# A wider spacing of threshold-search steps between the evictions of an in-projection

## Chip, core and metric

One NeuronCore of one Trainium2 chip runs the whole program. The metric is the device time of one execution in microseconds (us). Five engines matter. TensorE multiplies into PSUM. ScalarE and VectorE empty PSUM and do arithmetic, GpSimd does arithmetic on SBUF, and SyncE mostly issues transfers. Each engine executes its own instructions strictly in the order of its program, and semaphores are the only tie between engines: an instruction that waits holds up everything queued behind it on its engine.

## What is computed

One decoder layer on 1024 prompt tokens and 8 x 4 sample tokens. The part that the change touches is the in-projection `h @ w_in` and the choice of keys for sparse attention. The reference, cut:

```python
au, av, q, k, v, qi, ki, wi = jnp.split(h @ w_in, IN_SPLITS, axis=-1)
u = jax.nn.gelu(au); vg = layer_norm(jax.nn.gelu(av), a_ln_g, a_ln_b)
...
s = jax.nn.relu(jnp.einsum('bthd,bsd->bths', qi, ki_all))
score = jnp.einsum('bths,bth->bts', s, wi)
score = jnp.where(adm[None], score, -jnp.inf)
_, sel = lax.top_k(score, topk)          # topk = 256
```

The kernel doesn't sort. For each row of scores it looks for the threshold above which 256 keys lie, by 32 halvings, and turns the result into a mask.

## The kernel before

**Tiles and stages.** The prompt is cut into 8 tiles of 128 tokens (0 to 7), the 32 sample tokens are tile 8. The stage in question first makes the index projections and the scores of all tiles, and then projects tile after tile, in the order 8, 0, 1, ... 7 (`TURN`), by four groups of matmuls each: av (group 0), au (1), kv (2) and q (3). A group is 8 float32 products of 128x128 by 128x512 (16 rows of the profile), at L678, into one PSUM bank. Groups alternate between two banks, so group n+2 waits until ScalarE has evicted group n.

**Evictions, on ScalarE.** av goes to `vg` (L867), au to `u` (L873), kv to `k_nat` and `v_nat` (L878, L879), q to `mixT` (L884). ScalarE also evicts the spatial product `mix` of the tile before (`spat`, L904) and two transposes, `aT` and `kpost` (L785), and issues the loads of `ada_b` (L801) for a second product, `ada`, that runs in between (L708).

**GpSimd** normalises `vg` of each tile (the last line L565), multiplies `u` by `spat`, and rotates k and q. TensorE's `mix` of tile t (L691), one tile later, needs the normalised `vg` of t.

**The batched search.** The scores of tiles 2 to 7 are searched together. One step (`try`) needs both engines. VectorE counts the scores above the candidate `cand` for four tiles (L980), ScalarE does so for the other two with a Sign that accumulates (`near`, L896, two instructions, 128x768 and 128x1024). VectorE then waits for both counts, compares them with the bounds (L983), corrects (L984, L985) and writes the next candidate (L987), on which ScalarE's next Sign waits. So 32 steps are one serial chain. Behind it VectorE finishes the thresholds (`end`, L993 to L996) and turns the scores into masks (`pick`, 7 instructions for each of 6 tiles, L1004 to L1016). The attention stage's first VectorE instruction (L1097) stands behind all that.

**What sets the order.** A list `ORDER` is made once, and TensorE, ScalarE and VectorE each walk through it and emit their own part of every entry. For the stretch in question it is made from `LATE`, the groups and what belongs to them, by an account of time: `COST` adds 6.9 for a group, 2.0 for `mix`, 0.6 for `aT`, 0.4 for `kpost` and 1.0 for `ada`, and when the account holds enough for a step of the search, that step is put into the list there. These numbers only set the order; no engine waits for a time. TensorE has no part in `try`, `end` and `pick`.

Of the kernel before, what the change touches and what calls it, by code (L numbers as in the profile page):

```python
# [107 lines left out]
def step_kernel(nc, a, outs):  # L108
# [20 lines left out]
    with ExitStack() as keep, ExitStack() as tail:  # L129
# [117 lines left out]
        with ExitStack() as ctx:  # L247
# [85 lines left out]
            queue = [("try", 0, i) for i in range(SEARCH)] + [("end", 0, 0)]  # L333
            queue += [("pick", t, i) for t in range(2, TILES) for i in range(PICK)]
            began, time = False, 0.0
            for x in LATE:
                ORDER.append(x)
                began = began or x[0] == "ready"
                if began:
                    time += COST.get(x[0], 0.0)  # L340
                while queue and time >= (4.0 if queue[0][0] == "try" else 1.3):
                    time -= 4.0 if queue[0][0] == "try" else 1.3
                    ORDER.append(queue.pop(0))
            ORDER += queue + [("mix", TILES - 1, 0), ("kpost", TILES - 1, 0), ("aT", TILES - 2, 0)]
            NA = len(ORDER)
# [1894 lines left out]
```

How the kernel before makes its waits and increments, by code:

```python
                @block.sync  # L398
                def _(sp):
                    sp.dma_start(cnat[0:1, :], a["c_prompt"]).then_inc(s_c, 16)
                    sp.dma_start(cnat[1:1 + SEQS, :], a["c_sample"]).then_inc(s_c, 16)
                    sp.dma_start(const[:, :], a["table"]).then_inc(s_const, 16)
                    sp.wait_ge(s_z, 1)
                    for j in range(4):
                        sp.dma_start(modn[32 * j:32 * j + 1 + SEQS, 0, :],
                                     b_ada[j * 512:(j + 1) * 512].partition_broadcast(1 + SEQS)).then_inc(s_bada, 16)
# [9 lines left out]
                        sp.dma_start(bsp_s[s * DSEQ:(s + 1) * DSEQ, :],  # L416
                                     a["b_spatial"][0, :, 0:DSEQ].rearrange("h t -> t h"),
                                     allow_slow_non_contiguous=True).then_inc(s_sp, 16)
                    sp.dma_start(bsp[:, :], a["b_spatial"][0].rearrange("h t -> t h"),
                                 allow_slow_non_contiguous=True).then_inc(s_sp, 16)
                    sp.wait_ge(s_adamm, 1)
                    for t in range(2, TILES + 1):
                        sp.wait_ge(s_trf, tr_done(("h", t - 2, 1)))
# [8 lines left out]
                        sp.dma_start(new_kidx[t - 2], idx_nat[:, (t - 2) % 3, 256:320]).then_inc(s_sti[(t - 2) % 3], 16)  # L432
                    for t in (TILES - 1, TILES):
                        sp.wait_ge(s_roti, t + 1)
                        sp.dma_start(new_kidx[t], idx_nat[0:rows(t), t % 3, 256:320]).then_inc(s_sti[t % 3], 16)
```

## Time and profile before

| | us |
|---|---|
| plain runs | 1559.14, 1565.89, 1566.51 |
| median of these | 1565.89 |
| the profiled execution, its own time | 1561.62 |
| its span, first to last instruction | 1559.4 |
| TensorE busy in the span | 1414.2 (91%) |
| VectorE busy in the span | 570.0 (37%) |
| ScalarE busy in the span | 372.2 (24%) |
| GpSimd busy in the span | 326.5 (21%) |

All times in the rows are counted from the start of the span. The in-projection's groups run from about 125 to 400 us, the attention of the prompt follows until about 540, and the expert layer takes the second half. A busy share is an average over stages, so it doesn't tell which engine is waited for in a given one; idle times with what ended them, and the timelines, do.

### The profile page before, as it was taken

Reading aid. Unit: us, or ns where it says so; the run is one execution under the profiler, and the core shown is the slowest. Engines: PE = TensorE matmul, PEld = TensorE weight load, DVE = VectorE, ACT = ScalarE, POOL = GpSimd, SP = SyncE. Lnnn points to the kernel's source line nnn. Section 1 sums busy time; section 2 is a strip of 40 time slices with the busy share of each in tenths; the row PEclk is TensorE's granted clock in tenths of the full one; section 3 lists DMA queues with packets and bytes.
Section 4 is the critical chain, followed back from the end, with each engine's and each line's share of the span. In section 5 each row is a group of like instructions: output and inputs, shape, how many; then the busy total and the mean of one; then the engine's idle time right before and its main releaser. Section 6 shows DMA issues by size and latency. Waiting matters only on the chain. (4 is left out here: it accounts for less than half of the span.)

```text
span 1559.4 us, 25014 instructions
## 1 busy us (share of the span) xinstructions
PE 1414.2 (91%) x9464; PEld 671.2 (43%) x9464; DVE 570.0 (37%) x1266; ACT 372.2 (24%) x827; POOL 326.5 (21%) x495
## 2 busy tenths in 40 slices
PE   5989999999999899997289999999999999999955
PEld 2644444444466644453234444444444444444421
DVE  1246999970355448435810111011111011100129
ACT  1334555311466431111011111111111111111114
POOL 0217544596200014322000000000000000000037
PEclk8999999999899999998589999999999999999978
DMA  8808211221121163301869999999999999999845
GB/s 316 308 17 274 67 62 61 88 88 61 29 79 40 46 188 109 108 29 53 333 239 388 378 405 406 405 403 407 407 403 400 407 407 405 397 402 397 317 150 197
DMA packets 96366, 377.30 MB, mean 242 GB/s; under 512 B 19567, under 2 KB 37039, under 8 KB 82988
## 3 DMA queue, kind: packets, MB, share of 16 engines
q1 hardware_dynamic: 72924, 319.15, 53.0%
q10 hardware_dynamic: 16384, 32.52, 6.1%
q0 software_dynamic: 6992, 24.78, 5.1%
q8 instruction: 39, 0.64, 0.2%
q14 instruction: 27, 0.22, 0.0%
HBM read 340.59 MB, written 35.81 MB: 241 GB/s over the span
## 5 line engine op out<-in xcount | busy, mean ns | idle before, releaser
L1894 PE MATMUL psum<-wgu,xgT 128*32 128x256 f32 (+1 forms) x3840 | 428.7, 453 | 5.5 <-DMA wgu<-in_w_up_dram 4.6
L1894 PEld LDWEIGHTS psum<-wgu,xgT 128*32 128x32 f32 (+1 forms) x3840 | 170.6, 119 | 261.4 <-issue 212.3
L678 PE MATMUL psum<-w_sb,mixT 128*128 128x512 f32 x512 | 232.2, 607 | 10.4 <-ACT u L873 8.0
L1903 PE MATMUL psum<-wd,hidT 128*32 128x256 f32 (+1 forms) x1920 | 220.7, 454 | 0.0
L678 PEld LDWEIGHTS psum<-w_sb,mixT 128*128 128x128 f32 x512 | 96.6, 194 | 135.1 <-issue 113.5
L1943 POOL DMA_INDIRECT xg<-h_dram,tokens x33 | 30.4, 922 | 548.1 <-PE psum L1886 499.6
L1903 PEld LDWEIGHTS psum<-wd,hidT 128*32 128x32 f32 (+1 forms) x1920 | 79.7, 118 | 127.5 <-issue 101.0
L2057 DVE TENSOR_TENSOR hid<-silu,psum 128x256 f32<-128x256 f32 x40 | 16.9, 422 | 282.7 <-ACT silu L2003 282.7
L1453 PE MATMUL psum<-w_o,mixT 128*128 128x512 f32 x256 | 111.6, 594 | 1.1 <-PEq L1165 1.1
L980 DVE TENSOR_SCALAR_CACHE_REDUCE above<-bias,cand 128x384 int8<-128x384 f32 (+3 forms) x128 | 108.3, 846 | 4.6
L2003 ACT ACTIVATE silu<-psum 128x256 f32<-128x256 f32 x40 | 15.4, 384 | 325.5 <-PE psum L1894 325.5
L1453 PEld LDWEIGHTS psum<-w_o,mixT 128*128 128x128 f32 x256 | 48.1, 190 | 60.8 <-issue 60.8
L2078 DVE COPY yy<-psum 128x256 f32<-128x256 f32 x32 | 13.6, 424 | 157.5 <-PE psum L1903 157.5
L2059 DVE TENSOR_TENSOR hid<-silu,psum 128x128 f32<-128x128 f32 x40 | 11.5, 288 | 123.4 <-ACT silu L2005 123.4
L2166 PE MATMUL psum<-y,diag 128*128 128x512 f32 (+1 forms) x72 | 33.9, 626 | 22.3 <-DMA y<-ys_dram,slot 22.3
L1886 PE MATMUL psum<-const,xg 96*128 96x96 f32 x328 | 42.6, 273 | 11.6 <-DMA xg<-h_dram,tokens 11.6
L795 ACT ACTIVATE prob<-prob,nmin 128x128 f32<-128x128 f32 (+7 forms) x64 | 48.7, 766 | 0.0
L896 ACT ACTIVATE near<-bias,cand 128x768 int8<-128x768 f32 x32 | 29.9, 935 | 70.3 <-DVE cand L987 68.6
L1886 PEld LDWEIGHTS psum<-const,xg 96*128 96x128 f32 x328 | 40.0, 205 | 11.7 <-DMA xg<-h_dram,tokens 11.7
L2028 ACT ACTIVATE yy<-psum 128x512 f32<-128x512 f32 x32 | 19.1, 597 | 105.1 <-PE psum L1903 105.1
L633 PE MATMUL psum<-w_idx,mixT 128*128 128x324 f32 (+1 forms) x144 | 43.2, 455 | 0.0
L600 PE MATMUL psum<-const,prob 128*128 128x128 f32 x288 | 41.7, 284 | 0.9 <-ACT qT L916 0.2
(375 smaller groups left out, 1597.9 us busy)
## 6 DMA issues: line engine op xcount, KB each, us to landing
wgu<-in_w_gate_dram SPq DMA_DIRECT2D x40, 2048.0 KB, 17.7
wgu<-in_w_up_dram SPq DMA_DIRECT2D x40, 2048.0 KB, 22.7
wd<-in_w_down_dram SPq DMA_DIRECT2D x40, 2048.0 KB, 23.3
ada_b<-in_w_ada_dram ACTq DMA_DIRECT2D x16, 1024.0 KB, 4.9
ys_dram<-yy ACTq DMA_DIRECT2D x80, 128.0 KB, 8.4
ys_dram<-zero SPq DMA_DIRECT2D x22, 384.0 KB, 4.7
ada_a<-in_w_ada_dram SPq DMA_DIRECT2D x4, 2048.0 KB, 15.7
w_sb<-in_w_in_dram SPq DMA_DIRECT2D x4, 2048.0 KB, 10.1
```

Source lines behind the costliest of these rows:

```text
L600: last = nc.tensor.transpose(bank[BTB[n % 3]][:, col:col + P], src, c("ident"))
L633: last = nc.tensor.matmul(bank[2 + n % 2][0:r, 0:IDX_W], mixT[:, k, t * P:t * P + r], w_idx[:, k, :], start=(k == 0), stop=(k == DC - 1))
L678: last = nc.tensor.matmul(bank[2 + n % 2], mixT[:, k, t * P:(t + 1) * P], w_sb[:, k, n0:n0 + 512], start=(k == 0), stop=(k == DC - 1))
L795: s.activation(x, x, ACT.Exp, bias=nmin[:, e:e + 1], scale=-1.0, accum_out=den[:, e:e + 1]).then_inc(b_exp, 1)
L896: s.activation(near[:, n - ON_DVE, 0:(b + 1) * P], score_of(b), ACT.Sign, bias=cand[:, n:n + 1], scale=-1.0, accum_out=under[:, n:n + 1]). ...
L980: then(v.tensor_scalar(above[:, 0:(t + 1) * P], score_of(t), cand[:, n:n + 1], 0.0, ALU.is_lt, ALU.add, accum_out=under[:, n:n + 1]))
L1453: last = nc.tensor.matmul(out[half], mixT[:, k, t * P:(t + 1) * P], w_o[:, k, half * 512:(half + 1) * 512], start=(k == 0), stop=(k == DC ...
L1886: last = nc.tensor.transpose(bank[1 if k < 4 else 7][:, (k % 4) * CAP:(k % 4 + 1) * CAP], x[:, k, :], c("ident", CAP)[:, 0:CAP])
L1894: last = nc.tensor.matmul(out[m * j:m * j + m, 0:2 * w], xgT[:, b, k, first:first + m], wgu[:, b, :, k, w * j:w * j + w], start=(k == 0), ...
L1903: last = nc.tensor.matmul(out[m * j:m * j + m, 0:w], hT(k), wd[:, b, k, w * j:w * j + w], start=(k == 0), stop=(k == KD - 1))
L1943: nc.gpsimd.indirect_dma_start(out=xg[:, e % 2, :], out_offset=None, in_=h2_dram[:, :], in_offset=bass.IndirectOffsetOnAxis(ap=tokens[0:CA ...
L2166: last = nc.tensor.matmul(bank[2 * (t % 4) + half][0:r, :], diag[0:r, k, t, 0:r], y[0:r, t % 4, half * 512:(half + 1) * 512], start=(k == ...
```

## The change

The account must hold 5.5 instead of 4.0 before a step of the search is put into the list. The 1.3 of a `pick` instruction stay.

```diff
-                while queue and time >= (4.0 if queue[0][0] == "try" else 1.3):
-                    time -= 4.0 if queue[0][0] == "try" else 1.3
+                while queue and time >= (5.5 if queue[0][0] == "try" else 1.3):
+                    time -= 5.5 if queue[0][0] == "try" else 1.3
                     ORDER.append(queue.pop(0))
```

TensorE's, GpSimd's and SyncE's programs stay as they were. On ScalarE and VectorE the same instructions stand in another order.

First place: ScalarE, from the eviction of the av group of tile 2 (`vg`) to that of its au group (`u`). `near,under` is a Sign of the search, two of them a step; `spat` and `mixT` evict `mix` and `aT`. Before:

```order
L867 ACTIVATE vg<-psum 128x512
L801 DMA ada_b_63<-in_w_ada_dram 128x2048
L896 ACTIVATE near,under<-bias,cand 128x768
L896 ACTIVATE near,under<-bias_last,cand 128x1024
L896 ACTIVATE near,under<-bias,cand 128x768
L896 ACTIVATE near,under<-bias_last,cand 128x1024
L904 ACTIVATE spat<-psum 128x512
L785 ACTIVATE mixT<-psum 128x4x128
L873 ACTIVATE u<-psum 128x512
```

After, the same place:

```order
L867 ACTIVATE vg<-psum 128x512
L801 DMA ada_b_63<-in_w_ada_dram 128x2048
L896 ACTIVATE near,under<-bias,cand 128x768
L896 ACTIVATE near,under<-bias_last,cand 128x1024
L904 ACTIVATE spat<-psum 128x512
L896 ACTIVATE near,under<-bias,cand 128x768
L896 ACTIVATE near,under<-bias_last,cand 128x1024
L785 ACTIVATE mixT<-psum 128x4x128
L873 ACTIVATE u<-psum 128x512
```

Two steps stand between the two evictions in both, but they are steps 16 and 17 before and 10 and 11 after, and the second one now stands behind `spat`. From one au group to the next there are 8 steps before and 6 after.

Second place: ScalarE at the last steps of the search. Before, they are steps 30 and 31, behind the eviction of tile 4's av group:

```order
L896 ACTIVATE near,under<-bias,cand 128x768
L896 ACTIVATE near,under<-bias_last,cand 128x1024
L904 ACTIVATE spat<-psum 128x512
L785 ACTIVATE mixT<-psum 128x4x128
L873 ACTIVATE u<-psum 128x512
L785 ACTIVATE kT<-psum 128x2x128
L878 ACTIVATE k_nat<-psum 128x256
L879 ACTIVATE v_nat<-psum 128x256
L884 ACTIVATE mixT<-psum 128x2x128 x2
```

After, they are around the evictions of tile 5's au group (`u`) and kv group (`k_nat`, `v_nat`):

```order
L873 ACTIVATE u<-psum 128x512
L896 ACTIVATE near,under<-bias,cand 128x768
L896 ACTIVATE near,under<-bias_last,cand 128x1024
L785 ACTIVATE kT<-psum 128x2x128
L878 ACTIVATE k_nat<-psum 128x256
L879 ACTIVATE v_nat<-psum 128x256
L896 ACTIVATE near,under<-bias,cand 128x768
L896 ACTIVATE near,under<-bias_last,cand 128x1024
L884 ACTIVATE mixT<-psum 128x2x128 x2
```

The search ends five groups later in the order, and from there on ScalarE has evictions alone in both. On VectorE the addition that closes the first `ada` product (L1081) stands behind step 21, where it stood behind step 29; the second one stands behind the last `pick` in both.

## Rows read from the trace of the kernel before

**Rows 1.** The page, costliest groups: form xcount | busy, mean ns | idle before, releaser.

```profile
L678 PE MATMUL psum<-w_sb,mixT 128*128 128x512 f32 x512 | 232.2, 607 | 10.4 <-ACT u L873 8.0
```

**Rows 2.** Who waited for whom, 120 to 300 us: total us, times, longest.

```profile
ACT near L896 <- DVE cand L987: 68.6, 31, 4.3
```

**Rows 3.** ScalarE's timeline: start, us, instruction [idle before it, what ended it].

```profile
215.83 0.94 ACT L896 ACTIVATE near<-bias,cand 128x768 int8<-128x768 f32 x1 [2.87 <-DVE cand L987]
...
217.90 0.57 ACT L904 ACTIVATE spat<-psum 128x512 f32<-128x512 f32 x1
...
218.85 0.59 ACT L873 ACTIVATE u<-psum 128x512 f32<-128x512 f32 x1
...
376.19 0.60 ACT L867 ACTIVATE vg<-psum 128x512 f32<-128x512 f32 x1 [7.40 <-PE psum L678]
```

**Rows 4.** TensorE's timeline, some of its groups (x16) and the last mix.

```profile
168.10 7.13 PE L678 MATMUL psum<-w_sb,mixT 128*128 128x512 f32 x16
...
200.89 7.03 PE L678 MATMUL psum<-w_sb,mixT 128*128 128x512 f32 x16
...
219.50 8.83 PE L678 MATMUL psum<-w_sb,mixT 128*128 128x512 f32 x16 [2.39 <-ACT u L873]
...
256.79 8.83 PE L678 MATMUL psum<-w_sb,mixT 128*128 128x512 f32 x16 [2.38 <-ACT u L873]
...
294.91 8.68 PE L678 MATMUL psum<-w_sb,mixT 128*128 128x512 f32 x16 [3.21 <-ACT u L873]
...
313.66 7.03 PE L678 MATMUL psum<-w_sb,mixT 128*128 128x512 f32 x16
...
320.74 7.03 PE L678 MATMUL psum<-w_sb,mixT 128*128 128x512 f32 x16
...
345.91 7.03 PE L678 MATMUL psum<-w_sb,mixT 128*128 128x512 f32 x16
...
378.16 7.03 PE L678 MATMUL psum<-w_sb,mixT 128*128 128x512 f32 x16
...
401.27 2.00 PE L691 MATMUL psum<-vg,wspT 128*128 128x64 f32 x16
```

**Rows 5.** Busy us (xinstructions) of PE, PEld, DVE, ACT, POOL; granted clock; DMA share, GB/s.

```profile
290.00:300.00 10.00, 6.79 (x19) 2.44 (x18) 9.44 (x22) 4.43 (x10) 9.20 (x14) 0.83 0.00 0
300.00:310.00 10.00, 10.00 (x30) 4.05 (x29) 9.51 (x17) 0.66 (x2) 4.37 (x11) 1.00 0.40 131
```

**Rows 6.** Line 896: min/median/max ns, first and last start.

```profile
L896 ACT ACTIVATE near<-bias,cand x32: 934/935/936, 144.1 to 291.2; 128x768 int8<-128x768 f32 x32
```

**Rows 7.** VectorE's timeline: first scans of three steps, selection's first and last, attention's first.

```profile
148.62 0.61 DVE L980 TENSOR_SCALAR_CACHE_REDUCE above<-bias,cand 128x384 int8<-128x384 f32 x1
...
155.78 0.61 DVE L980 TENSOR_SCALAR_CACHE_REDUCE above<-bias,cand 128x384 int8<-128x384 f32 x1
...
160.14 0.61 DVE L980 TENSOR_SCALAR_CACHE_REDUCE above<-bias,cand 128x384 int8<-128x384 f32 x1
...
299.94 0.61 DVE L1004 TENSOR_SCALAR_CACHE_REDUCE above<-bias,cand 128x384 int8<-128x384 f32 x1
...
342.68 0.69 DVE L1016 TENSOR_SCALAR bias_last<-above 128x1024 f32<-128x1024 int8 x1
...
406.81 0.29 DVE L1097 CUSTOM_DVE_ANT_0 prob<-psum,causal 128x128 f32<-128x128 f32 x1 [3.92 <-PE psum L738]
```

**Rows 8.** GpSimd's timeline: first and last instruction of two normalisations.

```profile
312.42 0.97 POOL L511 TENSOR_TENSOR tmp<-vg 128x256 f32<-128x256 f32 x1 [4.84 <-ACT vg L867]
...
331.74 1.99 POOL L565 TENSOR_TENSOR vg<-vg,aln_b 128x512 f32<-128x512 f32 x1
...
345.14 0.73 POOL L511 TENSOR_TENSOR tmp<-vg 128x256 f32<-128x256 f32 x1
...
357.50 1.27 POOL L565 TENSOR_TENSOR vg<-vg,aln_b 128x512 f32<-128x512 f32 x1
```

## The prediction

> **What bounds the kernel now.** The profiled execution took 1561.62 us, of which the span is 1559.4 us; the three plain runs have a median of 1565.89 us (1559.14 to 1566.51). I read the page first. TensorE is busy 91% of the span, and the in-projection's matmuls (L678) show 10.4 us of idle time before them, 8.0 us of it ended by ScalarE's write of u (L873) [rows 1]. An input of a matmul group is never that late: what TensorE waits for is a PSUM bank, since groups alternate between two banks and group n+2 may start only when group n is evicted. So ScalarE is late, and the next view says why: its Sign instructions of the search (L896) stood waiting 68.6 us, 31 times, for the candidate that VectorE writes at L987 [rows 2]. ScalarE executes in order, and an eviction queued behind such a Sign waits with it.
>
> The timelines show one case. The au group of tile 2 ends on TensorE near 207.9 us. ScalarE does the second of two search steps at 215.83, after 2.87 us of waiting, then spat, mixT and at last u at 218.85, over 10 us after the group ended [rows 3]. TensorE's next group but one starts at 219.50 after 2.39 us of idle time, and takes 8.83 us where an unstalled one takes 7.0 to 7.13 us [rows 4]. The excess is the clock: in the 10 us around the third such stall the granted clock is 0.83, and 1.00 in the 10 us behind it, with TensorE busy for all 10 [rows 5].
>
> The price of it all is best taken from whole tiles, as the sum of idle time and slow clock. From one au group to the next TensorE needs 32.25 us when nothing is late (345.91 to 378.16, and 313.66 to 345.91 as well). From the au group of tile 1 (168.10) to that of tile 5 (313.66), four tiles, it took 145.56 us, where 4 x 32.25 is 129.00 [rows 4]. **Excess: 16.56 us.** Outside these four tiles no group of the stage shows an eviction wait. The listed idle time is 10.4 us; two groups of 8.83 us and one of 8.68 us against 7.13 us add 4.95; some 0.2 us at each refill is the rest.
>
> Why the queue falls behind: a search step costs VectorE 4.36 us when nothing disturbs it (155.78 to 160.14), and on average (291.2 - 144.1) / 31 = 4.75 us [rows 6, 7]. The old order puts 8 steps into a tile: 8 x 4.75 = 38.0 us of a serial chain beside 32.25 us of matmuls. The chain is the bound there, not TensorE.
>
> **The change, part by part.** Nothing is added or removed: 32 steps, 42 selection instructions and all evictions stay; TensorE, GpSimd and SyncE have the same rows in the same order. Only the places on ScalarE and VectorE move.
>
> *Fewer steps for each tile.* The cost 5.5 makes 6 steps for each tile instead of 8 (counted in the order from au group to au group). 6 x 4.75 = 28.5 us, below 32.25. So the chain has 3.7 us to spare in each tile and cannot accumulate a lag. Locally, at most two steps stand between the evictions of two groups. One step takes ScalarE 215.83 to 217.90, 2.07 us [rows 3]. If both candidates had to be waited for in full, the two would take 2 x 4.75 = 9.5 us; the first usually is ready, because VectorE runs its own scans while ScalarE waits for the matmul. The eviction may be up to a whole group (7.0 us) late before TensorE notices. I therefore price the leftover at 0.6 us, the size of the small waits, and the bounds at 0 and 6 us (one stall of the 2.39 + 1.70 us kind and something small). Gain: 16.56 - 0.6, some **16 us**.
>
> *Steps come later.* The last step moves from behind the av group of tile 4 to behind the kv group of tile 5. That eviction's matmuls start at 320.74 now [rows 4], so end near 327.7, and near 311.2 after the gain; two instructions of eviction, Sign and the closing operations, and the selection starts near 317 instead of 299.94. It lasts from 299.94 to 342.68 plus 0.69, 43.4 us [rows 7], and would end near 361. The first VectorE instruction that has to stand behind it is the attention stage's at 406.81 [rows 7], 390.2 after the gain. So 29 us of cover remain, where there are 63 before. The move costs nothing by itself, and a microsecond for each microsecond beyond those 29.
>
> *The ada operation of VectorE* (L1081) comes after step 21 rather than step 29. It waits for the product that TensorE issues right behind the q group of tile 3; steps 20 and 21 stand behind that group's eviction on ScalarE, so it is done by the time. No wait is added.
>
> *The selection collides with other GpSimd work.* While VectorE selects, GpSimd is slower: its normalisation takes 312.42 to 333.73 = 21.3 us beside the selection and 345.14 to 358.77 = 13.6 us without [rows 8]. Now it hits tile 5, then it will hit tile 6 and perhaps the start of tile 7. For tile 6: start near 327.3, done near 348.6, and TensorE wants the result near 359. For tile 7: eviction at 376.19 now [rows 3], near 360.2 then; even the full 21.3 us end at 381.5, and the product that needs it starts at 401.27 now, 384.7 then [rows 4]. So 3 us are left in the worst case and 10 in the likely one. Cost: nothing.
>
> The Trainium skill has a rule that speaks against this move: in "SBUF — State Buffer", section "SBUF: two separate sides", VectorE and GpSimd share one port pair as an exclusive lock, taken for a whole instruction, by a VectorE instruction with two SBUF inputs too. The trace agrees in kind: GpSimd lost 21.3 against 13.6 us. If the 7.7 us that the lock took from one normalisation were paid at the stage's end, the gain would be 8 us instead of 16; by the rows they lie under cover.
>
> *Behind the stage* all engines meet at a barrier, and each later load is released by work of this core, so what the stage gives is handed on one to one.
>
> **Sum.** 1561.62 - 16 = 1545.6 us on the profile's footing; 1565.89 - 16 = 1549.9 us on the median's. The three runs scatter by 7 us and the profile lies between, so I take the middle, **1547.5 us**, 1.0% less.
>
> **The rivals.**
> 1. *Evictions stay late in places.* The order is laid out with 6.9 us for a group; steps still stand in pairs at the q groups. For it: some steps take far longer than the mean; the second ran from 148.62 to 155.78, 7.16 us [rows 7]. Against it: the tolerated 7.0 us and 3.7 us of slack in a tile. Price: one stall (2.39 + 1.70 us) in two or three tiles, 4 to 12 us back: 1552 to 1559 us. Chance 0.09.
> 2. *GpSimd becomes late at the end.* If the selection's lock hits both tile 6 and tile 7 in full and tile 6's rotations push tile 7's start, mix of tile 7 waits. Tile 6's whole GpSimd work took 312.42 to 345.14, 32.7 us [rows 8]; from 327.3 it ends at 360.0, just when tile 7's input arrives. Price: 0 to 5 us, 1548 to 1553 us. Chance 0.05. The port-pair rule of the page above works in this direction.
> 3. *No change: the clock takes it.* If a TensorE that never pauses were granted less, 0.93 over the 240 us would cost 17 us. Against it: 1.00 with TensorE busy for 10.00 of 10 us behind the last stall [rows 5]. About 1562 us. Chance 0.05.
> 4. *Slower: the search overruns the stage.* Place: VectorE before the first attention scores. It costs from the point where the selection ends after 390.2, and makes the kernel slower than before only if it ends after 406.8, 46 us later than I work out. The steps would have to take over 9 us each, against a mean of 4.75 [rows 6]. 2 us late would read 1568 us. Chance 0.03, with all that I haven't seen.
>
> **How the numbers follow.** Forecast 0.78, rivals 0.09, 0.05, 0.05, 0.03. 0.5% is 7.8 us, about what a measurement of this kernel can tell. Faster by more: 0.78 + 0.05 + half of rival 1 = 0.88; within 0.5%: 0.09; slower 0.03. Range: the forecast's own is 1559.14 - 16.6 = 1542.5 (lowest run, full gain) to 1549.9 plus scatter; I go to 1541 below, and to 1556 above, which takes in rival 2 and most of rival 1.
>
> **What would show it.** In the profile after: no idle time ended by L873, L867 or L879 before L678; the au groups 32.2 to 32.4 us apart from tile 1 to tile 7; granted clock 1.00 from 150 us to the stage's end; the first scores near 390 us instead of 406; Sign's first and last starts near 144 and 312. Steps: selection from 315 to 320 until about 361, and GpSimd's slow normalisation at tile 6. Wrong would be: idle time before L691 ended by GpSimd (rival 2), a first attention row released by L1016 (rival 4), or a granted clock under 1.00 without gaps (rival 3).

## The result and the profile after

The changed kernel took 1542.8 us (median of 4 runs, 1538.02 to 1547.61) against 1564.63 us for the kernel before (4 runs, 1559.14 to 1566.51) in the same comparison. The ratio is 0.9878, with a 95% interval of 0.985 to 0.9905. Two later comparisons of the same pair gave 0.9933 (0.9906 to 0.996) and, with the most runs, 0.9894 (0.987 to 0.9918). The two profiled executions differ by 17.2 us (1561.62 to 1544.46). So the change is worth about 1%, some 16 us; the forecast was 1547.5 us, in a range of 1541 to 1556.

The page after, the line that answers to [rows 1]: matmuls x512 of the in-projection | busy, mean ns | idle before.

```profile
L678 PE MATMUL psum<-w_sb,mixT 128*128 128x512 f32 x512 | 227.0, 596 | 0.0
```

The idle time fell from 10.4 us to 0.0, and busy time by 5.2 us (232.2 to 227.0) for the same 512 rows: that is the slow clock gone, which the idle column doesn't show. The waits between 120 and 300 us, as in [rows 2]:

```profile
ACT vg L867 <- PE psum L678: 20.5, 6, 5.4
ACT near L896 <- DVE cand L987: 19.8, 13, 3.4
...
DVE miss L983 <- ACT near L896: 13.8, 8, 3.7
```

ScalarE's Sign waited 19.8 us in place of 68.6. ScalarE now waits for TensorE's groups, as it should where TensorE is the bound, and there is a new wait in the opposite sense: VectorE's L983 waits for the Sign, which stands behind an eviction. It costs nothing here, since no group of the stage waits for an eviction any more. In the kernel before, VectorE never waited for a Sign in this stretch: its view of waits has no such row. So the 4.75 us of a step were VectorE's own work, and ScalarE's 2.07 us of it never set the pace. TensorE's timeline, for comparison with [rows 4]: the same au groups, tile 1, 2 and 5 to 7, and the last mix product.

```profile
166.76 7.13 PE L678 MATMUL psum<-w_sb,mixT 128*128 128x512 f32 x16
...
199.11 7.03 PE L678 MATMUL psum<-w_sb,mixT 128*128 128x512 f32 x16
...
295.87 7.03 PE L678 MATMUL psum<-w_sb,mixT 128*128 128x512 f32 x16
...
328.13 7.03 PE L678 MATMUL psum<-w_sb,mixT 128*128 128x512 f32 x16
...
360.38 7.03 PE L678 MATMUL psum<-w_sb,mixT 128*128 128x512 f32 x16
...
383.49 2.00 PE L691 MATMUL psum<-vg,wspT 128*128 128x64 f32 x16
```

From the au group of tile 1 to that of tile 5 it takes 129.11 us where it took 145.56: 16.45 us less. From there to the last mix product it takes 87.62 us (before 87.61). Neither of the two groups behind tile 2's au group waits any more. ScalarE at that place, for [rows 3]; columns start, duration, [idle before, what ended it]:

```profile
200.69 0.94 ACT L896 ACTIVATE near<-bias,cand 128x768 int8<-128x768 f32 x1 [0.43 <-DVE cand L987]
...
202.75 0.57 ACT L785 ACTIVATE mixT<-psum 128x512 f32<-128x512 f32 x1
206.18 0.60 ACT L873 ACTIVATE u<-psum 128x512 f32<-128x512 f32 x1 [2.85 <-PE psum L678]
```

The group starts at 199.11 and ends near 206.1; `u` is written at 206.18, at once, where it came more than 10 us after its group. (The two steps ahead of this eviction in the kernel before are steps 14 and 15, counted from 0 like the others, and not 16 and 17.) The later parts of the work, on VectorE, for [rows 7]:

```profile
357.25 0.69 DVE L1016 TENSOR_SCALAR bias_last<-above 128x1024 f32<-128x1024 int8 x1
383.70 1.41 DVE L1081 SCALAR_TENSOR_TENSOR modn<-psum,modn 64x512 f32<-64x512 f32 x2 [25.75 <-PE psum L708]
389.03 0.29 DVE L1097 CUSTOM_DVE_ANT_0 prob<-psum,causal 128x128 f32<-128x128 f32 x1 [3.92 <-PE psum L738]
```

The selection is done at 357.94, and VectorE then stands idle for 25.75 us until TensorE's product: the cover that is left. Attention's first VectorE instruction comes at 389.03 instead of 406.81. GpSimd's two normalisations, for [rows 8], now of tiles 6 and 7:

```profile
326.89 1.07 POOL L511 TENSOR_TENSOR tmp<-vg 128x256 f32<-128x256 f32 x1 [4.74 <-ACT vg L867]
...
346.30 1.99 POOL L565 TENSOR_TENSOR vg<-vg,aln_b 128x512 f32<-128x512 f32 x1
...
359.70 0.72 POOL L511 TENSOR_TENSOR tmp<-vg 128x256 f32<-128x256 f32 x1
...
372.03 1.26 POOL L565 TENSOR_TENSOR vg<-vg,aln_b 128x512 f32<-128x512 f32 x1
```

21.4 us beside the selection and 13.6 us without it, as before, one tile later.

### The profile page after: what moved, and what is told of

It is laid out like the page before. It is cut to its first block and busy times, and to the rows that moved or that the text cites. A ratio compares the mean times of both kernels' runs of the same rounds, so it can differ in the third digit from the quotient of the medians.

```text
span 1542.2 us, 25014 instructions
## 1 busy us (share of the span) xinstructions
PE 1405.9 (91%) x9464; PEld 667.2 (43%) x9464; DVE 572.6 (37%) x1266; ACT 371.7 (24%) x827; POOL 324.3 (21%) x495
## 5 line engine op out<-in xcount | busy, mean ns | idle before, releaser
L1894 PE MATMUL psum<-wgu,xgT 128*32 128x256 f32 (+1 forms) x3840 | 429.2, 453 | 5.6 <-DMA wgu<-in_w_up_dram 4.7
L1894 PEld LDWEIGHTS psum<-wgu,xgT 128*32 128x32 f32 (+1 forms) x3840 | 170.9, 119 | 261.8 <-issue 212.7
L678 PE MATMUL psum<-w_sb,mixT 128*128 128x512 f32 x512 | 227.0, 596 | 0.0
L2078 DVE COPY yy<-psum 128x256 f32<-128x256 f32 x32 | 13.6, 424 | 157.5 <-PE psum L1903 157.5
L2005 ACT ACTIVATE silu<-psum 128x128 f32<-128x128 f32 x40 | 11.1, 277 | 129.2 <-PE psum L1894 129.2
```

The costliest lines, as they stand in the source:

```text
L678: last = nc.tensor.matmul(bank[2 + n % 2], mixT[:, k, t * P:(t + 1) * P], w_sb[:, k, n0:n0 + 512], start=(k == 0), stop=(k == DC - 1))
L1894: last = nc.tensor.matmul(out[m * j:m * j + m, 0:2 * w], xgT[:, b, k, first:first + m], wgu[:, b, :, k, w * j:w * j + w], start=(k == 0), ...
```

## The theories and the experiments

**Rate theory** (the prediction's): the 32 steps are a serial chain on VectorE and ScalarE, 4.75 us each. Where the order asks for more of them in a tile than fit beside its 32.25 us of matmuls, ScalarE falls behind and evictions come late. **Placement theory**, its rival: what counts is that evictions stand ahead of a threshold wait, however many waits there are. A third question is where the wider spacing begins to cost: **the overrun** of the selection into the attention stage.

The kernel before already bears the rate theory out. With rows 4, these two au groups (tiles 3 and 4) give the time of each tile:

```profile
238.40 7.03 PE L678 MATMUL psum<-w_sb,mixT 128*128 128x512 f32 x16
...
275.70 7.03 PE L678 MATMUL psum<-w_sb,mixT 128*128 128x512 f32 x16
```

From 200.89 on, the tiles take 37.5, 37.3 and 38.0 us, where 8 x 4.75 is 38.0. The first one, 168.10 to 200.89, takes only 32.8: the lag has to build up first. And the step's mean is above its undisturbed 4.36 us in part because small VectorE instructions are slow while GpSimd normalises (209.07 to 222.77 for tile 2), 0.69 and 1.12 us in place of 0.17:

```profile
214.36 0.69 DVE L983 TENSOR_TENSOR miss<-under,const 128x6 f32<-128x6 f32 x1
...
220.31 1.12 DVE L985 TENSOR_TENSOR low<-low,miss 128x6 f32<-128x6 f32 x1
```

One measure serves for all kernels: the time from the start of tile 1's au group to that of the last mix product. It leaves out what differs at a run's start (that au group starts between 165.7 and 170.2 us) and behind the stage.

### The same rate, later in the order

The account starts with a debt of 8, so each step stands two steps later, still 8 in a tile:

```diff
-            began, time = False, 0.0
+            began, time = False, -8.0
```

> The old spacing of 4.0, but the account starts at -8.0, so that every step of the search stands two steps later in the order, with more evictions ahead of it, at the same 8 steps a tile. Rate theory: the chain of 4.75 us steps is still longer than a tile's matmuls, the lag builds up as before from a later start, and the last mix product stays within 2 us of 401.3 us. Placement theory (what counts is that evictions come ahead of a threshold wait, not how many waits there are): most of the stalls go, and the mix product comes near 385 to 390 us.

TensorE's timeline of this kernel:

```profile
254.45 7.13 PE L678 MATMUL psum<-w_sb,mixT 128*128 128x512 f32 x16 [2.38 <-ACT u L873]
...
298.68 9.66 PE L678 MATMUL psum<-w_sb,mixT 128*128 128x512 f32 x16 [9.33 <-ACT u L873]
...
406.03 2.00 PE L691 MATMUL psum<-vg,wspT 128*128 128x64 f32 x16
```

Its tile 1 au group started at 170.17, 2.07 us later than in the profile before, so the measure is 235.86 us against 233.17: worse by 2.7 us. The mix product was expected within 2 us of 401.3; it came 4.8 us later, 2.7 us by the measure, so the rate theory's own number was missed too. The total ratio is 1.002 (1.0 to 1.0039). Moving the steps later at the old rate brings nothing. The last stall grows to 9.33 us: three steps now stand between the evictions of tile 4's av and au groups (before `spat`, two; between `mixT` and `u`, one more). So placement does count for the size of a single stall. And since two steps still stand behind nearly every group, this kernel tests one other placement, not all of them; the next two experiments leave the order alone.

### The old order with a shorter chain

Only VectorE's fourth scan is cut, to 128 of 896 columns, so tile 6's threshold isn't the reference's:

```diff
+                            w = P if n == ON_DVE - 1 else (t + 1) * P
-                            then(v.tensor_scalar(above[:, 0:(t + 1) * P], score_of(t), cand[:, n:n + 1], 0.0, ALU.is_lt, ALU.add,
+                            then(v.tensor_scalar(above[:, 0:w], score_of(t)[:, 0:w], cand[:, n:n + 1], 0.0, ALU.is_lt, ALU.add,
                                                  accum_out=under[:, n:n + 1]))
```

> The old order with spacing 4.0; the one change is that VectorE's fourth scan of a step (tile 6, 896 columns, 1.15 us) counts only the first 128 columns, so that tile 6's threshold isn't the reference's. A step should fall from 4.36 to about 3.5 us bare and 3.9 us in the mean. Rate theory: 8 x 3.9 = 31 us is under 32.25, so the stalls go with the order untouched, and the last mix product comes near 385 us (from 401.3). Placement theory: the order is what it was, so at least half of the 16.6 us excess stays (mix product at 393 or later).

The bare step, between the first scans of two steps on VectorE (line numbers are one higher in this kernel):

```profile
180.99 0.61 DVE L981 TENSOR_SCALAR_CACHE_REDUCE above<-bias,cand 128x384 int8<-128x384 f32 x1
...
184.56 0.61 DVE L981 TENSOR_SCALAR_CACHE_REDUCE above<-bias,cand 128x384 int8<-128x384 f32 x1
```

And TensorE's in-projection matmuls between 140 and 400 us, with their idle time:

```profile
L678 PE MATMUL psum<-w_sb,mixT 128*128 128x512 f32 x481 | 213.3, 596 | 0.0
```

3.57 us bare; the mean, from the first scan of the first step (142.68) to that of the last (269.29), is 4.08 us, where 3.9 was expected. All stalls are gone, with the order untouched; the measure is 216.73 us, the same to the hundredth as with the new order. The ratio is 0.9889 (0.9832 to 0.9946). The placement theory expected at least half of the excess to stay; it falls here. Note that 8 x 4.08 = 32.7 us is still slightly over 32.25: a lag of 0.4 us a tile is forgiven by the second bank.

### The new order with a longer chain

The opposite: spacing 5.5, but the fourth scan done twice.

```diff
+                            for _ in range(2 if n == ON_DVE - 1 else 1):
```

> The new order (spacing 5.5) with VectorE's fourth scan of each step done twice, so a step costs 1.2 us more: about 5.5 us bare, 5.9 us in the mean; nothing else differs and the values are the same. Rate theory: 6 x 5.9 = 35.4 us is over 32.25, so lag builds up again by 3 us a tile and, after the first 7 us of it, stalls come back in the last two or three tiles of the search: 3 to 10 us, last mix product at 387 to 394 us. Placement theory: the new order keeps evictions ahead of the waits, no stalls, mix product near 383.5 us.

```profile
247.60 7.13 PE L678 MATMUL psum<-w_sb,mixT 128*128 128x512 f32 x16 [0.34 <-ACT u L873]
...
284.10 10.16 PE L678 MATMUL psum<-w_sb,mixT 128*128 128x512 f32 x16 [4.18 <-ACT u L873]
...
391.94 2.00 PE L691 MATMUL psum<-vg,wspT 128*128 128x64 f32 x16
```

A step takes 5.99 us in the mean (first scans from 143.51 to 329.12), and 6 of them 35.9 us. The stalls come back with the new order: 0.34 and 4.18 us of waiting and 3.03 us of slow clock in one group (10.16 against 7.13). Tiles 1 and 2 show none, the wait at tile 3 is the short one and that at tile 4 the long one, though the steps stand much alike in each tile: the lag adds up. The measure is 224.40 us, 7.7 over the stall-free one, so about half of the stage's gain is lost. The ratio is 0.9934 (0.9909 to 0.9959).

### Sweeping the spacing

In each of these kernels the two numbers 4.0 become the one named.

```diff
-                while queue and time >= (4.0 if queue[0][0] == "try" else 1.3):
-                    time -= 4.0 if queue[0][0] == "try" else 1.3
+                while queue and time >= (4.5 if queue[0][0] == "try" else 1.3):
+                    time -= 4.5 if queue[0][0] == "try" else 1.3
```

**4.5.**

> Spacing 4.5, so 7.2 steps a tile on average. Rate theory: 7.2 x 4.75 = 34.4 us against 32.25, a lag of 2.1 us a tile that adds up to about 9 us over the search, against some 7 us that the second bank forgives: 0 to 3 us of stalls left, mix product at 384 to 387 us. If instead the stalls go only when the chain fits inside a tile, half of the excess stays and it comes at 391 or later.

```profile
279.58 7.13 PE L678 MATMUL psum<-w_sb,mixT 128*128 128x512 f32 x16 [1.14 <-ACT u L873]
...
290.65 7.13 PE L678 MATMUL psum<-w_sb,mixT 128*128 128x512 f32 x16 [2.94 <-ACT v_nat L879]
```

Stalls of 1.14 and 2.94 us are left, at the end of the search, where the lag has accumulated. That is 1 us more than the 0 to 3 expected (and the mix product, at 387.40, is just outside 384 to 387), but a quarter of the old excess, as a lag of 2.1 us a tile with a forgiving second bank would have it.

**4.75.**

> Spacing 4.75, 6.9 steps a tile: 6.9 x 4.75 = 32.6 us against 32.25, a lag of 0.3 us a tile, 1.5 us over the whole search and far inside what the second bank forgives. Rate theory: no eviction wait, from the au group of tile 1 to the last mix product 216.7 us as at 5.0 and 5.5, where 4.5 took 220.9 and 4.0 took 233.2.

No eviction wait; 386.81 - 170.09 = 216.72 us. The total is one run, so only its trace counts.

**5.0.**

> Spacing 5.0, 6.5 steps a tile: 6.5 x 4.75 = 30.9 us. No stall, mix product near 383.5 us as with 5.5, and the same time within 0.3%. Its search should end near 303 us in place of 313, which leaves VectorE idle earlier and costs nothing.

No eviction wait; the measure is 216.73 us, the last mix product at 383.67. VectorE's first instruction behind the search starts at 302.15 (313.68 with 5.5). The ratio is 0.9895 (0.9865 to 0.9924).

**6.5.**

> Spacing 6.5. The last step comes near 347 us, and the last 9 of 42 selection instructions now stand behind VectorE's closing addition of the second ada product, which waits for TensorE until near 383.5 us. Theory: no stall in the stage's groups, but the selection ends near 396 us, so the first attention scores (L1097) start near 397 instead of 389: 7 to 8 us of the gain are gone, total 8 to 10 us under before. Rival (the cover is larger than I think, since the first tiles' attention needs no mask): the time equals spacing 5.5.

No eviction wait. The ratio is 0.9945 (0.9922 to 0.9968), some 8.6 us under before, as expected; the overrun is read below, with that of 7.0.

**7.0.**

> Spacing 7.0. The last step comes near 362 us, and 22 of 42 selection instructions stand behind the second ada addition: 384.9 us plus about 28 us, so attention's first VectorE instruction starts near 413 instead of 389, 24 us late and 7 us later than in the kernel before. Theory: slower than before by 5 to 9 us (ratio 1.003 to 1.006), with no eviction stall at all in the in-projection; the overrun of the selection, not the stalls, is then the price. Rival: attention catches up, and the time stays under before's.

VectorE's timeline at 7.0, around the second ada addition:

```profile
384.33 1.41 DVE L1081 SCALAR_TENSOR_TENSOR modn<-psum,modn 64x512 f32<-64x512 f32 x2 [2.02 <-PE psum L708]
385.77 0.49 DVE L1016 TENSOR_SCALAR bias<-above 128x640 f32<-128x640 int8 x1
...
409.49 0.69 DVE L1016 TENSOR_SCALAR bias_last<-above 128x1024 f32<-128x1024 int8 x1
410.22 0.29 DVE L1097 CUSTOM_DVE_ANT_0 prob<-psum,causal 128x128 f32<-128x128 f32 x1
```

The rest of the selection stands behind L1081, and attention's first VectorE instruction follows on its last one at 410.22 with no wait for TensorE: the chain has passed over to VectorE. At 6.5 that instruction starts at 395.3, 12.8 us after the mix product, where 5.5 us is usual: 7.3 us of overrun, as expected. At 7.0 it is 26.1 us after it, 20.6 us of overrun; I had expected 24. Compared with the kernel before, attention starts 3.4 us later (410.22 to 406.81), 4.1 us counted from tile 1's au group. The ratio of 1.0017 (0.9999 to 1.0036) allows that, but doesn't tell it from no change; 5 to 9 us slower had been expected. So the overrun of rival 4 is real, while a kernel slower than before isn't shown.

The third column is the time from the start of the last mix product to attention's first VectorE instruction.

| spacing | measure, us | mix to attention, us | ratio (95% interval) |
|---|---|---|---|
| 4.0 (before) | 233.17 | 5.54 | 1 |
| 4.0, debt of 8 | 235.86 | 5.55 | 1.002 (1.0 to 1.0039) |
| 4.5 | 220.94 | 5.55 | 0.9924 (0.9896 to 0.9952) |
| 4.75 | 216.72 | 5.55 | one run, 1548.17 us |
| 5.0 | 216.73 | 5.54 | 0.9895 (0.9865 to 0.9924) |
| 5.5 (the change) | 216.73 | 5.54 | 0.9878, 0.9933, 0.9894 |
| 6.5 | 216.72 | 12.80 | 0.9945 (0.9922 to 0.9968) |
| 7.0 | 216.73 | 26.10 | 1.0017 (0.9999 to 1.0036) |

### How large the gain is

> The changed kernel once more, beside its comparison partners on one chip. The rate theory (the old order asks for 8 serial steps a tile, 38.0 us, beside 32.25 us of matmuls) expects what the first profile showed: no eviction wait before L678, the last mix product near 383.5 us, 15 to 20 us less than before in all. If the total gain beyond the stage's 16.4 us is scatter of runs, this comparison comes out nearer to 16.5 us (ratio 0.989 to 0.990); if something behind the stage gains too, nearer to 20 us (0.987).

> Spacing 5.5 with more rounds, since two comparisons gave 0.9878 and 0.9933. In the traces the in-projection's last mix product comes 16.4 us earlier counted from the same au group, in both profiles alike; theory: that is the whole effect and the ratio comes out at 0.9885 to 0.991. If something behind the stage gained as well, it would be 0.987 or less.

> Spacing 5.0 beside 5.5 on the same chip. Theory: TensorE doesn't wait for an eviction in either, so the two agree within 0.2%. If the longer idle stretch of VectorE or the earlier selection mattered, they'd differ by more.

The first repeat had 0.9933, a smaller gain than either alternative had allowed, and its interval (0.9906 to 0.996) doesn't meet that of the first comparison (0.985 to 0.9905). So comparisons of this pair scatter by more than their intervals say. The second, with more runs, had 0.9894, which is 0.0106 x 1560.8 = 16.5 us, and its traced measure is again 216.72 us (385.42 - 168.70). The stage's gain is thus 16.4 us in every trace, and that is the whole effect as far as the traces show one. The differences between the comparisons lie outside it, and their place isn't found. The expert layer's gate and up matmuls (L1894) ran from 766.1 to 1462.7 us in one profile of the changed kernel and from 765.6 to 1458.5 us in the other, 696.6 against 692.9 us, and took 696.0 us in the kernel before (786.3 to 1482.3). That scatter of 3.7 us is part of it, but less than half of the 8.6 us between 0.9878 and 0.9933. Spacing 5.0 beside 5.5 on the same chip: 0.991 (0.9884 to 0.9935) against 0.9894, medians of 1545.8 and 1543.75 us. The two agree within 0.2% and their intervals overlap.

## Why the prediction was right, point by point

- **What bounds the stage.** Right, by two experiments that leave the order alone and change the chain: shorter chain, no stalls in the old order; longer chain, stalls in the new one. In the kernel before VectorE alone sets the chain's pace, as the waits show.
- **The price of the stalls, 16.56 us.** 16.44 us measured (233.17 to 216.73), idle time and slow clock together. Reading the idle column alone would have given 10.4.
- **The leftover, 0.6 us.** It was 0.0. The slack of 3.7 us a tile was more than was needed; the sweep puts the edge between 4.5 (stalls left) and 4.75 (none).
- **Steps come later at no cost.** Selection from 314.47 to 357.94, forecast 317 to 361; cover left 25.75 us before the ada addition and 31 us before the first scores, forecast 29. The sweep shows where it ends: 7.3 us of overrun at 6.5. VectorE's first ada addition, at 261.54, came without a wait. (The search ends six groups later in the order, from tile 4's av to tile 5's kv group, and not five; the times forecast were worked out from the right group.)
- **How far the overrun is away.** Rival 4 says that the steps would have to take over 9 us each to make the kernel slower. That sum is wrong: a search of 31 steps from 144 us that ends 46 us later than near 313 has steps of (359 - 144) / 31 = 6.9 us. At spacing 7.0 the first scans start 6.81 us apart in the mean (143.36 to 354.58), and attention starts later than in the kernel before. The rival was nearer than its reason said.
- **GpSimd beside the selection.** Tile 6's normalisation from 326.89 to 348.29, forecast 327.3 to 348.6; tile 7's was done at 373.29, over 10 us before the mix product wanted it. Rival 2 had no part. The Trainium skill's exclusive port pair ("SBUF — State Buffer", "SBUF: two separate sides") fits the 21.4 us beside the selection, against 13.6 without it; no run isolates the ports. The loss lay under cover and still does, one tile later.
- **The clock.** Rival 3 falls: in each 10 us from 150 to 380 us TensorE is busy for 10.00 and the granted clock is 1.00. From 290 to 300 us it was 0.83 before [rows 5]:

```profile
290.00:300.00 10.00, 10.00 (x39) 5.62 (x39) 9.41 (x27) 6.30 (x14) 4.65 (x10) 1.00 0.33 105
```

- **The sum.** 1547.5 forecast, 1542.8 measured, a miss of 4.7 us. The stage's term was off by 0.4 us. The first comparison's medians differ by 21.8 us, 5.4 more than the stage gives, and no trace shows where: the expert layer's matmuls took 696.6 us against 696.0 before. The forecast was for 16, which the repeats bracket with 0.9933 and 0.9894. That the first comparison's median still lies inside the range, near its lower end, owes something to luck.

## What to carry to other kernels

Where a serial chain across two engines is threaded between evictions, compare its steps in a tile times the step's mean time (not the undisturbed one) with the bound engine's time for that tile. At spacing 4.5, 7.2 x 4.36 = 31.4 us would have fitted into 32.25, and 4.1 us of waits were left; 7.2 x 4.75 = 34.4 us doesn't fit. A small excess over few tiles is forgiven, as at 4.75 and in the short chain. If the excess is larger, spread the chain over more tiles, until the work that waits for its end comes out from under cover; the one other placement tried here at the old rate didn't help. By the stage's measure 4.75, 5.0 and 5.5 are equally good, and both edges were foreseen to within a few microseconds.

## What the runs showed that was not expected

A stall's price in clock doesn't follow from its length. In the kernel before, waits of 2.38, 2.39 and 3.21 us were each followed by a group of 8.68 to 8.83 us instead of 7.13 [rows 4]. At spacing 4.5 a wait of 2.94 us, and in the kernel with the debt one of 2.38 us, were followed by an undisturbed group of 7.13 us. The granted clock says the same: between 290 and 300 us the kernel at spacing 4.5, with the group that had waited 2.94 us, has 1.00.

```profile
290.00:300.00 10.00, 9.35 (x37) 5.52 (x38) 9.30 (x28) 4.34 (x11) 4.46 (x14) 1.00 0.51 155
```

What decides it is left open by these runs. For an estimate, only the time over whole tiles counts both parts.
